# Trainium2: one 256-wide product per token for the PEER routing weights, their low halves on GpSimd

## The reference, cut to what matters

```python
s = einsum('thpd,hpnd->thpn', q, sub_keys)
s1, i1 = top_k(s[:, :, 0], 16);  s2, i2 = top_k(s[:, :, 1], 16)
cand, cand_id = s1[..., :, None] + s2[..., None, :], i1[..., :, None] * 128 + i2[..., None, :]
top, pos = top_k(cand, 16)                       # per token and head; 8 heads
eid = take_along_axis(cand_id, pos)              # 128 experts per token
g = softmax(top)                                 # 128 weights per token
act = gelu(einsum('td,ted->te', xb, u[eid]))
return einsum('te,ted->td', g * act, v[eid])
```

## Time and profile before

| | us |
|---|---|
| median of 3 runs | 3054.89 |
| the profiled execution, its own time | 3056.21 |
| its span, first to last instruction | 3054.4 |
| first and last token product (L897), both layers | 525.3 and 1941.9 |
| TensorE matmul busy (L-numbers are lines of the kernel) | 2840.4 (93%) |
| VectorE busy | 1996.3 (65%) |
| ScalarE busy | 1467.9 (48%) |
| GpSimd busy | 340.0 (11%) |

### The profile page before, as it was taken

One profiled execution on the slowest core, in us unless ns is written; L12 is line 12 of the kernel. 1 busy time (PEld: TensorE's weight loads), 2 busy tenths in 40 slices (PEclk: granted clock), 3 DMA queues, 4 the chain that ended last, 5 costly groups with the idle time before them and its releaser, 6 DMA issues.

```text
span 3054.4 us, 57292 instructions
## 1 busy us (share of the span) xinstructions
PE 2840.4 (93%) x19570; PEld 2644.3 (87%) x19570; DVE 1996.3 (65%) x4265; ACT 1467.9 (48%) x2414; POOL 340.0 (11%) x167
## 2 busy tenths in 40 slices
PE   6889899999999998878899999999999789999998
PEld 6878788999988887867899999988887679998998
DVE  6545961888466666686579687557776676556655
ACT  4444344444455555454444444445555454445443
POOL 0002676000000000000079200000000000000000
PEclk9999899999999999889999999999999899999999
DMA  3434356445666664323345545666666324551454
GB/s 150 166 138 152 132 194 215 172 173 172 231 243 240 241 241 176 125 83 133 116 165 197 186 173 175 209 239 242 240 240 230 131 80 161 187 221 70 162 183 166
DMA packets 140448, 546.15 MB, mean 179 GB/s; under 512 B 15784, under 2 KB 81592, under 8 KB 83616
## 3 DMA queue, kind: packets, MB, share of 16 engines
q1 hardware_dynamic: 63216, 455.38, 41.4%
q10 hardware_dynamic: 73728, 67.14, 7.1%
q0 software_dynamic: 3376, 21.88, 1.9%
HBM read 505.53 MB, written 40.91 MB: 179 GB/s over the span
## 4 chain that ended last, share of the span: by engine, by line
PE 74%; DVE 9%; DMA 6%; ACT 4%; POOL 4%; issue 3%; ACTq 0%; SPq 0%; DVEq 0%
PE bank L709 22%; PE bank L710 22%; PE bank L711 21%; POOL wL L503 4%; PE bank L897 4%; ACT wH L493 3%; DMA act_parked<-act_out 3%; DMA ring<-in_w_stream 3%; DVE wL L503 2%; PE bank L793 1%; PE bank L815 1%; DVE act_out L1574 1%; PE bank L806 1%; DVE h L1598 1%; PE bank L722 1%
## 5 line engine op out<-in xcount | busy, mean ns | idle before, releaser
L503 DVE TENSOR_TENSOR wL<-ring,wH 128x1024 fp32r<-128x1024 f32 x744 | 909.5, 1225 | 768.4 <-ACT wH L493 767.6
L709 PE MATMUL bank<-hnH,wH 128*128 128x256 f32 x3648 | 1062.1, 291 | 57.2 <-DVE hnL L1556 31.0
L493 ACT ACTIVATE wH<-ring 128x1024 fp32r<-128x1024 f32 x864 | 909.3, 1055 | 335.5 <-DMA ring<-in_w_stream 157.0
L710 PE MATMUL bank<-hnL,wH 128*128 128x256 f32 x3648 | 1043.9, 286 | 0.0
L711 PE MATMUL bank<-hnH,wL 128*128 128x256 f32 x3648 | 1043.1, 286 | 0.0
L709 PEld LDWEIGHTS bank<-hnH,wH 128*128 128x128 f32 x3648 | 711.8, 195 | 69.0 <-issue 45.1
L710 PEld LDWEIGHTS bank<-hnL,wH 128*128 128x128 f32 x3648 | 712.6, 195 | 0.1
L711 PEld LDWEIGHTS bank<-hnH,wL 128*128 128x128 f32 x3648 | 710.9, 195 | 0.0
L709 PE MATMUL bank<-wH,wgtH 128*128 128x512 f32 x1024 | 399.4, 390 | 5.0 <-issue 4.5
L710 PE MATMUL bank<-wL,wgtH 128*128 128x512 f32 x1024 | 399.0, 390 | 0.0
L711 PE MATMUL bank<-wH,wgtL 128*128 128x512 f32 x1024 | 398.9, 390 | 0.0
(11 more groups left out here) (347 smaller groups left out, 3432.1 us busy)
## 6 DMA issues: line engine op xcount, KB each, us to landing
ring<-in_w_stream SPq DMA_DIRECT2D x432, 1024.0 KB, 4.9
act_parked<-act_out ACTq DMA_DIRECT2D x256, 128.0 KB, 3.6
act_in<-act_parked ACTq DMA_DIRECT2D x256, 128.0 KB, 2.7
sw_bias<-in_c_swa POOLq DMA_DIRECT2D x1, 4096.0 KB, 14.1
relb_rows<-rel_table POOLq DMA_DIRECT2D x1, 2048.0 KB, 9.6
h_parked<-h POOLq DMA_DIRECT2D x2, 1024.0 KB, 6.3
h_back<-h_parked POOLq DMA_DIRECT2D x2, 1024.0 KB, 6.6
od_relb<-relb_rows POOLq DMA_DIRECT2D x2, 1024.0 KB, 8.0
```

The costliest lines, as they stand in the source:

```text
L493: eng.activation(wH[:, b % NBUF, :], raw(b), ACT.Copy).then_inc(w_high, 1)
L503: eng.tensor_tensor(wL[:, b % NBUF, :], raw(b), wH[:, b % NBUF, :].bitcast(F32), ALU.subtract).then_inc(w_low, 1)
L709: pe.matmul(dst, lh, rh, start=start, stop=False, skip_group_check=True)
L710: pe.matmul(dst, lh, rl, start=False, stop=False, skip_group_check=True)
```

## The change

- The two one-hot tables become fp32r. `second` holds the one-hot rows of the second index; `first_by_gate` holds the one-hot rows of the first index twice, once times the high part of the weight (fp32r), once times the low part (`gate_hl`). `tokens` is one fp32r matmul per token with 256 columns, high and low sheet side by side.
- `tokens` goes by pairs of tokens: one pair in the middle of `acts`, one behind it. A quad's four tokens have two banks, of which there are two sets; the table buffers hold two pairs.
- VectorE makes `second` for two tokens by one TENSOR_TENSOR comparison, and `first_by_gate` by one SCALAR_TENSOR_TENSOR per token, all 128x256. It waits for each pair's predecessor but one.
- ScalarE copies the high sheets to `gates` (`gated`, semaphore `g_half`); VectorE then adds the low sheets from PSUM (`gated` on VectorE, 128x512) and frees the banks (`g_read`).
- `POOLED` becomes 40 + 64 + 3: the 64 `split_low` of the quads go from VectorE to GpSimd.
- Ahead of the quads, ScalarE copies the weights rounded to fp32r into `gate_hl` and VectorE subtracts for the low part.

```diff
--- before.py
+++ after.py
@@ -82,7 +82,8 @@
 ATT_LAG_PT, ATT_LAG_O = 2, 5
 DEEP = 4
 AHEAD = 40
-POOLED = AHEAD + 3
+POOLED = AHEAD + T // 4 + 3
+PAIRS = T // 2
 LEAD = 3
 
 
@@ -390,7 +391,8 @@
 
 
         (sq,) = stage(("sq", [DC, T], F32))
-        (onehot,) = stage(("onehot", [16, P], F32))
+        second, first_by_gate, gate_hl = stage(("second", [4, P], F32R), ("first_by_gate", [4, 2, P], F32R),
+                                               ("gate_hl", [2, T], F32R))
         act_in, wgtH, wgtL = stage(("act_in", [4, T], F32), ("wgtH", [2, T], F32R), ("wgtL", [2, T], F32R))
         sb("shared", [P, DC * T])
 
@@ -408,7 +410,8 @@
         small = sb("small", [P, 96])
         eps = small[:, 80:81]
         lbv = sb("lbv", [P, 24])
-        psum = [ctx.enter_context(nc.psum_tensor(f"bank{i}", [P, 512], F32)) for i in range(ALL_BANKS)]
+        banks = ctx.enter_context(nc.psum_tensor("banks", [P, ALL_BANKS, 512], F32))
+        psum = [banks[:, i, :] for i in range(ALL_BANKS)]
         psacc = psum[BANKS:]
         rel_dram = nc.dram_tensor("rel_table", [8, 512], F32, kind="Internal").ap()
         relb_dram = nc.dram_tensor("relb_rows", [P, 8, 512], F32, kind="Internal").ap()
@@ -423,6 +426,11 @@
 
         def V(name, c):
             return vec[:, VOFF[name] + c:VOFF[name] + c + 1]
+
+        def four_tokens(j):
+
+            first = BANKS + 2 * j % BANKS
+            return banks[:, first:first + 2, :].rearrange("p b (t h n) -> p n h (b t)", t=2, h=2)
 
         def spread(ap, axis, n):
 
@@ -460,6 +468,7 @@
         ho_sq_s, silu_s, hg_y = sem("ho_squares"), sem("hg_silu"), sem("hg_y")
         ckv_sq_s, ckvn_s, rel_used = sem("ckv_sq"), sem("ckvn"), sem("rel_used")
         cq_sq_s, mla_n, mla_qk, ff_low = sem("cq_sq"), sem("mla_normed"), sem("mla_qk"), sem("ff_low")
+        gate_high, g_half = sem("gate_high"), sem("g_half")
         eps_set, sink_set = sem("eps_set"), sem("sink_set")
         out_done, ffd_done = sem("out_done"), sem("ffn_down_block_done")
 
@@ -874,7 +883,7 @@
                 def evacuated(b):
                     pe.wait_ge(read_by[reader[held[b]]], rank[held[b]])
 
-                def acts(i, c):
+                def acts(i, c, between=None):
                     if isinstance(i, int) and 4 * i + c < BANKS:
                         evacuated(c)
                     else:
@@ -884,18 +893,20 @@
                     for k in range(DC):
                         last = product(psum[c % BANKS][:, 0:T], both(blk, FULL, slice(k * P, (k + 1) * P)),
                                        both(hn, FULL, k), k == 0, k == DC - 1)
+                        if between and k == DC // 2 - 1:
+                            tokens(*between)
                     last.then_inc(u_done, 1)
 
                 def tokens(i, j):
-                    if not isinstance(i, int):
-                        pe.wait_ge(g_read, i * 4 + (l * T // 4 + j + 1 - BANKS))
+                    if not isinstance(i, int) or j >= BANKS:
+                        pe.wait_ge(g_read, i * 4 + (l * T // 4 + j // 2 - 1))
                     elif j >= NT:
                         evacuated(BANKS + j)
-                    pe.wait_ge(onehots, i * 4 + (l * T // 4 + j + 1))
-                    for m in range(4):
-                        k = (4 * j + m) % 8
-                        last = pe.matmul(psacc[j][:, m * P:(m + 1) * P], onehot[:, k, :], onehot[:, 8 + k, :],
-                                         start=True, stop=True)
+                    pe.wait_ge(onehots, i * 8 + (l * PAIRS + j + 1))
+                    for m in range(2):
+                        k = (2 * j + m) % 4
+                        last = pe.matmul(psacc[j % BANKS][:, m * 2 * P:(m + 1) * 2 * P], second[:, k, :],
+                                         first_by_gate[:, k].rearrange("p a b -> p (a b)"), start=True, stop=True)
                     last.then_inc(g_done, 1)
 
                 def outs(i, c):
@@ -923,12 +934,12 @@
                         last = pe.transpose(ps[:, k * P:(k + 1) * P], src.rearrange("p a b -> p (a b)"), ident)
                     last.then_inc(group_done, 1)
                 for j in range(4):
-                    acts(0, AHEAD + j)
-                    tokens(0, j)
+                    acts(0, AHEAD + j, (0, 2 * j))
+                    tokens(0, 2 * j + 1)
                 with pe.Fori(1, T // 16) as i:
                     for j in range(4):
-                        acts(i, AHEAD + j)
-                        tokens(i, j)
+                        acts(i, AHEAD + j, (i, 2 * j))
+                        tokens(i, 2 * j + 1)
                 with pe.Fori(0, (N_KEYS - AHEAD - T // 4) // 4) as i:
                     for j in range(4):
                         acts(i, AHEAD + T // 4 + j)
@@ -1312,9 +1323,9 @@
 
                 def gated(i, j):
 
-                    act.wait_ge(g_done, i * 4 + (l * T // 4 + j + 1))
-                    act.activation(gates[:, :, bass.ds(i * 16 + 4 * j, 4)],
-                                   psacc[j][:, :].rearrange("p (t n) -> p n t", t=4), ACT.Copy).then_inc(g_read, 1)
+                    act.wait_ge(g_done, i * 8 + (l * PAIRS + 2 * j + 2))
+                    act.activation(gates[:, :, bass.ds(i * 16 + 4 * j, 4)], four_tokens(j)[:, :, 0, :],
+                                   ACT.Copy).then_inc(g_half, 1)
 
                 def acts_back(i, c):
 
@@ -1342,6 +1353,7 @@
                     acted(0, AHEAD - 4 + j)
                 for tt in range(NT):
                     ps = take((p + "slotT", tt))
+                    act.activation(gate_hl[:, 0, tt * P:(tt + 1) * P], ps[:, 0:P], ACT.Copy).then_inc(gate_high, 1)
                     act.activation(slotT[:, :, tt * P:(tt + 1) * P], ps[:, 0:3 * P].rearrange("p (a b) -> p a b", a=3),
                                    ACT.Copy).then_inc(read_by["act"], 1)
 
@@ -1715,17 +1727,28 @@
                 read_of(dve, (p + "slotT", 1))
                 b0 = BNO[(p + "u", 0)]
 
+                for tt in range(NT):
+                    dve.wait_ge(gate_high, NT * l + tt + 1)
+                link(dve.tensor_tensor(gate_hl[:, 1, :], slotT[:, 0, :], gate_hl[:, 0, :].bitcast(F32), ALU.subtract))
+
                 def rows(i, j):
-                    if not isinstance(i, int) or j >= 2:
-
-                        dve.wait_ge(g_done, i * 4 + (l * T // 4 + j - 1))
-                    for m in range(4):
-                        k = (4 * j + m) % 8
-                        tok = i * 16 + (4 * j + m)
-                        dve.tensor_scalar(onehot[:, k, :], iota, slotT[:, 2, bass.ds(tok, 1)], None, ALU.is_equal)
-                        last = dve.tensor_scalar(onehot[:, 8 + k, :], iota, slotT[:, 1, bass.ds(tok, 1)],
-                                                 slotT[:, 0, bass.ds(tok, 1)], ALU.is_equal, ALU.mult)
+
+                    pair = 2 * j % 4
+                    dve.tensor_tensor(second[:, pair:pair + 2, :], spread(iota, 1, 2),
+                                      spread(slotT[:, 2, bass.ds(i * 16 + 2 * j, 2)], 2, P), ALU.is_equal)
+                    for m in range(2):
+                        k = pair + m
+                        tok = i * 16 + (2 * j + m)
+                        last = dve.scalar_tensor_tensor(
+                            first_by_gate[:, k], spread(iota, 1, 2), slotT[:, 1, bass.ds(tok, 1)],
+                            gate_hl[:, :, bass.ds(tok, 1)].bitcast(F32).broadcast_to([P, 2, P]), ALU.is_equal, ALU.mult)
                     last.then_inc(onehots, 1)
+
+                def gated(i, j):
+
+                    four = gates[:, :, bass.ds(i * 16 + 4 * j, 4)]
+                    dve.wait_ge(g_half, i * 4 + (l * T // 4 + j + 1))
+                    dve.tensor_tensor(four, four_tokens(j)[:, :, 1, :], four, ALU.add).then_inc(g_read, 1)
 
                 def weigh(i, c):
 
@@ -1739,16 +1762,24 @@
                     dve.tensor_tensor(wgtL[:, c % 2, :].unsqueeze(1), gates[:, bass.ds(i * 4 + c, 1), :],
                                       wgtH[:, c % 2, :].bitcast(F32).unsqueeze(1), ALU.subtract).then_inc(wgt_low, 1)
 
-                for j in range(4):
-                    rows(0, j)
-                    split_low(dve, b0 + POOLED + j)
+                rows(0, 0)
+                rows(0, 1)
+                for j in range(1, 4):
+                    for k in (2 * j, 2 * j + 1):
+                        dve.wait_ge(g_done, l * PAIRS + k - 1)
+                        rows(0, k)
+                    gated(0, j - 1)
                 with dve.Fori(1, T // 16) as i:
                     for j in range(4):
-                        rows(i, j)
-                        split_low(dve, b0 + POOLED + j, i)
+                        for k in (2 * j, 2 * j + 1):
+                            dve.wait_ge(g_done, i * 8 + (l * PAIRS + k - 1))
+                            rows(i, k)
+                        gated(i, j - 1)
+                gated(0, T // 4 - 1)
+                dve.wait_ge(w_low, b0 + POOLED)
```

(2 more changed lines are left out.)

## The result

The kernel after takes **3211.31 us** (median of 4 runs, 3206.24 to 3216.13); beside it the kernel before took 3059.11 us (4 runs). The ratio is 1.0491 (95% interval 1.0443 to 1.0538): it is slower by 4.9%. Forecast were 3220 us, 3100 to 3320.

The account below looks back on a forecast made before the run. Before, TensorE bounds the quads; after, VectorE with GpSimd, taking turns at SBUF, 2.86 + 2.15 = 5.01 us a quad. 3056.2 + 160 + 5 = 3221, median of runs 1.3 lower: 3220 us, range 3100 to 3320.

Parts of the forecast that it names:

- TensorE's pace before (3.76) and its new form (3.36): TensorE's time per quad: 3.76 us before, with fp32 token products; 2.88 + 0.48 = 3.36 us with fp32r products.
- VectorE's own work, 2.86 us: VectorE's new instructions per quad: two comparisons, four SCALAR_TENSOR_TENSOR and the low-sheet addition, 2 x 0.33 + 4 x 0.40 + 0.60.
- Comparison and SCALAR_TENSOR_TENSOR take turns with GpSimd, the addition from PSUM does not: In the quads, VectorE instructions with two SBUF tensors alternate whole with GpSimd's low half, losing 2.15 us per low half.
- The walk: Step-by-step timeline of two quads: GpSimd takes its turns at 3.5 and 7.0 us, TensorE waits 1.0 and 2.1 us.
- 5.01 us a quad: Quad length with VectorE and GpSimd as the bound, without overlap: 2.86 + 2.15, against 3.76 before.
- The turn: Time GpSimd's low half takes from VectorE by holding SBUF access, taken as 2.15 us once per quad.
- Start of the quads, +5 us: Ahead of each layer's quads: two more ScalarE copies, a subtraction and a half block, perhaps one GpSimd turn; +2.5 a layer.
- Sum: Whole kernel: 128 x (5.01 - 3.76) = +160 us in the quads, plus 5 at their starts.
- The clock rival: TensorE's waits in the quads drop its clock to 1.2 GHz, a quad 5.97 us; 3281 to 3343 us; chance 0.07.
- TensorE near 65% of a quad: Expected sign in the profile after: TensorE busy near 65% of a quad of about 5 us, waiting for `first_by_gate`.

## Why the prediction was right, point by point

- **TensorE's pace before (3.76) and its new form (3.36).** Right. Before measured 3.78, and the two runs in which VectorE keeps up reach 3.37 and 3.38. The token products are 0.12 apart.
- **VectorE's own work, 2.86 us.** Right: the run with the low halves back on it gives 3.96, less 1.14 for the low half 2.82.
- **Comparison and SCALAR_TENSOR_TENSOR take turns with GpSimd, the addition from PSUM does not.** Right for all three, and the form for which there was no row went with its nearest row.
- **The walk.** In the timeline above quads start at 588.70 and 593.69, 4.99 apart, with the two turns where the walk had them: one on an S of the second pair, the next on an S of the first pair, 3.43 us later (the walk: 3.5).
- **5.01 us a quad.** Close to the 4.92 measured, but partly by luck. The forecast was 2.86 + 2.15, with no wait of VectorE. The runs give 2.86 + 1.85 + 0.21 = 4.92. The turn is 0.30 too large in the sum, since 53 turns fell partly beside the addition. The wait of 0.21 was put at nothing: VectorE waited 17.6 us for tokens and 9.5 us for ScalarE's copy, over 128 quads. The two errors cancel in part.
- **Start of the quads, +5 us.** 7.4 us lie outside the quads, but not as 2.5 a layer: the first copy of layer 0 starts at 527.5 in both kernels, 5.3 us came before layer 1's quads and 2.1 behind them. In layer 1 TensorE waited 7.1 us for its first tables, before at most 3.5; the subtraction that makes `gate_hl` was itself held there, by the turn that the forecast had left as possible. Timeline rows of after (GpSimd, then VectorE):

```profile
1769.75 4.64 POOL L512 TENSOR_TENSOR wL<-ring,wH 128x1024 fp32r<-128x1024 f32 x2 [0.38 <-ACT wH L502]
...
1772.07 2.60 DVE L1732 TENSOR_TENSOR gate_hl<-slotT,gate_hl 128x256 fp32r<-128x256 f32 x1 [8.61 <-ACT slotT L1357]
```

- **Sum.** 126 steps x (4.92 - 3.78) = 143, with 7 from outside the 150 us by which the spans differ; forecast were 165. The number was 9 us high: the turn's overlap with the addition took off more than VectorE's waits added.
- **The clock rival.** It occurred, but little: PEclk is 0.94 in the window shown above. From 597.0 to 600.5 it was 0.51, the lower level of 1.2 GHz, after TensorE had waited 0.83 and 1.90 us for tables; matmuls were 0.21 apart, as in the earlier trace rows. Behind that stretch VectorE, the bound, waited for tokens:

```profile
600.89 0.43 DVE L1737 TENSOR_TENSOR second<-con,slotT 128x256 fp32r<-128x256 f32 x1 [1.04 <-PE banks L908]
```

In the run with the turn at the addition, with regular waits of 1.1 us and 77 to 78% busy, the clock stayed at 1.00 in both windows looked at, and there VectorE's waits for tokens and copy are 8.5 us in both layers instead of 27.1. So the clock may have had a part in the 27.1 us; what these excursions cost by themselves was not tried. The price in the forecast is slightly off: 28 matmuls 0.21 apart are 5.9 us, not 5.97.
- **TensorE near 65% of a quad.** A miss: 46.65 of 60 us are 78%. A matmul's record is longer than its distance to the next; 346 of them 0.12 apart would be 41.5 us, 69%. How much of the rest is the slower clock was not taken apart.
- **One premise of the runs was too broad.** The forecast's sum has no TENSOR_SCALAR in it, but the first set of runs took all one-input forms as free of turns, and two expectations fell with it. The trace of before had the sign: a CAST of 256 elements with a minimum of 293 ns and a median of 2368.

## What to carry to other kernels

Before work goes to an idle GpSimd, look at what VectorE reads meanwhile. From SBUF with two tensors, or with TENSOR_SCALAR (and casts, by the trace of before), it stands still for nearly the whole of GpSimd's instruction, here some 2.1 us beside a step of 3.4 us. Reading one operand from PSUM takes VectorE out of it, for nothing in the two-tensor forms and for 0.06 to 0.07 us in TENSOR_SCALAR; a bank and one copy turned a loss of 4.9% into a gain of 1.4%. Where that cannot be had, a turn that fits into VectorE's waits and PSUM work costs almost nothing, so shorter GpSimd instructions can gain more than in proportion, as they did here.

## What the runs showed that I had not expected

- TENSOR_SCALAR from SBUF takes turns too (2560 and 2592 ns at most beside GpSimd), with fp32 data of 128 elements.
- Halving GpSimd's instruction (1.34 us instead of 2.41) took away not half of the loss but all of it, down to TensorE's own pace.
- GpSimd itself hardly suffers among short VectorE instructions: from 560 to 740 us of after its instruction has a mean of 2.45 us, against 2.41 undisturbed. The delay is nearly all on the other side.
